# First attention by head with rounded scores and value products, its output product in two rounded halves, and a rounded convolution output

## The reference, cut to what matters

```python
h = rms_norm(x, g_mix);  u = h @ w_in                      # split: u_f, u_q, u_kv, u_kr
y_f = fourier_mix(u_f, w_fourier)                          # 1024 x 512
q = rms_norm(u_q) @ w_q_up                                 # 8 heads of 96 (32 of them rotated)
k, v = rms_norm(u_kv) @ w_kv_up, with the rotated u_kr     # 8 heads of 96 and of 64
s = q @ k.T * scale;  p = softmax(s);  o = p @ v           # per head, 1024 x 1024 scores
x = x + concat([y_f, o], -1) @ w_out                       # 1024 x 1024
x = x + memory_cross_attention(...);  x = x + expert_choice_moe(...);  x = rms_norm(x)
```

```python
u = glu_a * sigmoid(glu_b);  u = conv31(u) + b
u = silu(layernorm(u));  y_conv = (u * silu(z_conv)) @ w_conv_out
merged = sigmoid(g_conv) * y_conv + sigmoid(g_att) * y_att
x = x + gate * (merged @ w_o);  return rms_norm(x)
```

## Time and profile before

| | |
|---|---|
| median of 3 runs | 3215.53 us (3215.28 to 3217.62) |
| the profiled execution | 3215.87 us |
| its span | 3214.1 us |
| mean granted TensorE clock | 0.976 of full speed |
| busy: PE, DVE, ACT, POOL | 94%, 53%, 32%, 15% |
| first attention, first score product to last output product | 298.6 to 714.7 us |
| four groups of `yc` products | from 2932.6 to 3107.8 us, 27.47 us each |

### The profile page before, as it was taken

One profiled execution on the slowest core, in us unless ns is written; L12 is line 12 of the kernel. 1 busy time (PEld: TensorE's weight loads), 2 busy tenths in 40 slices (PEclk: granted clock), 3 DMA queues, 4 the chain that ended last, 5 costly groups with the idle time before them and its releaser, 6 DMA issues.

```text
span 3214.1 us, 34166 instructions
## 1 busy us (share of the span) xinstructions
PE 3034.9 (94%) x13636; PEld 2197.6 (68%) x13636; DVE 1701.7 (53%) x2367; ACT 1033.3 (32%) x1640; POOL 475.7 (15%) x426
## 2 busy tenths in 40 slices
PE   6999999989999899999996896999999999999998
PEld 3566666656466448888885684887877768676568
DVE  2323323321023278888885589677778966111144
ACT  2123323221021037777775300334343343000001
POOL 1310000000000121121113423000001144121031
PEclk9999999999999899999998897999999999999999
DMA  3011000012011289999996111002021131011121
GB/s 120 27 54 53 1 1 1 1 66 105 27 53 46 102 318 382 397 391 398 397 392 234 66 60 58 8 11 89 14 89 31 31 102 51 28 49 44 40 105 66
DMA packets 136985, 362.22 MB, mean 113 GB/s; under 512 B 11119, under 2 KB 43377, under 8 KB 136700
## 3 DMA queue, kind: packets, MB, share of 16 engines
q1 hardware_dynamic: 120860, 305.30, 25.2%
q0 software_dynamic: 14672, 50.48, 4.9%
...
...
## 4 chain that ended last, share of the span: by engine, by line
PE 84%; DVE 11%; ACT 1%; issue 1%; POOL 1%; DMA 1%; SPq 0%; POOLq 0%; DVEq 0%; ACTq 0%
PE ps L1899 29%; PE ps L1885 6%; PE ps L2157 5%; PE ps L2159 5%; PE ps L2158 5%; DVE b_f L1667 5%; PE ps L2172 5%; PE ps L2173 5%; PE ps L2174 5%; PE ps L1998 3%; PE ps L2009 3%; PE ps L2227 3%; PE ps L2228 2%; PE ps L2229 2%; PE ps L2263 2%
## 5 line engine op out<-in xcount | busy, mean ns | idle before, releaser
L1667 DVE SCALAR_TENSOR_TENSOR b_f<-b_f,small_f 128x1023 f32<-128x1023 f32 (+14 forms) x210 | 309.9, 1476 | 7.6 <-DVE small_f L1765 1.2
L1899 PE MATMUL ps<-w_f,ht_f 128*128 128x512 f32 (+1 forms) x768 | 299.0, 546 | 0.0
L1899 PEld LDWEIGHTS ps<-w_f,ht_f 128*128 128x128 f32 x768 | 168.4, 231 | 115.0 <-issue 88.5
L1899 PE MATMUL ps<-w_f,b_f 128*128 128x512 f32 (+1 forms) x544 | 235.0, 586 | 12.5 <-DVE x_f L1516 6.2
L1899 PEld LDWEIGHTS ps<-w_f,b_f 128*128 128x128 f32 x544 | 102.6, 193 | 130.9 <-issue 109.2
L2158 PE MATMUL ps<-w_f32r,a_f32r 128*128 128x512 f32 x456 | 177.9, 390 | 0.0
L2172 PE MATMUL ps<-x_f32r,w_f32r 128*128 128x512 f32 x416 | 164.8, 396 | 0.0
L2173 PE MATMUL ps<-ht_f32r,w_f32r 128*128 128x512 f32 x416 | 162.5, 391 | 0.0
L2174 PE MATMUL ps<-x_f32r,w_f32r 128*128 128x512 f32 x416 | 162.4, 390 | 0.0
L1885 PE MATMUL ps<-small_f 128*128 128x128 f32 (+1 forms) x728 | 106.4, 293 | 59.1 <-DVE small_f L1415 39.7
L1129 ACT ACTIVATE b_f<-ps,small_f 128x1024 f32<-128x1024 f32 x64 | 71.3, 1113 | 275.0 <-DVE small_f L1500 275.0
...
## 6 DMA issues: line engine op xcount, KB each, us to landing
...
```

The costliest lines, as they stand in the source:

```text
L1667: ins = v.scalar_tensor_tensor(C[:, k, d:S], U[k][:, 0:S - d], cols[:, k, R_TAP + j:R_TAP + j + 1], C[:, k, d:S], ALU.mult, ALU.add)
L1899: ins = mm(o, lhs(k), rhs(k), start=(k == 0), stop=(k == n - 1))
```

## The change

Steps of the first attention become n = 8h + t, head by head, and its products rounded:

- Scores are three rounded passes for each half of 512 keys; hi and lo of Q and K of the next head are made in the loop, hi by ACT at t = 2 and 4 (`head_hi`), lo by POOL at t = 3 and 5 (`head_lo`).
- DVE takes a reciprocal of the row sum in each step, and POOL multiplies the probabilities (128 x 1024, in place) by it before PE turns them. ACT copies the turned probabilities as hi, DVE subtracts for lo, two of 512 columns each.
- The value product serves two query tiles at once: 16 rounded matmuls of 256 columns with the 128-wide pair (V hi, V lo) of a head stationary; the two halves of the result are added by an ACT copy (`o_half`) and a DVE addition into `mixa`. ACT makes hi (`mix_hi`) and POOL (the last quarter DVE) lo of `mixa`; hi and lo of the attention half of the output weights are made in the loop by ACT and POOL at i = 34 to 41.
- The output product is cut: `y1f`, the Fourier half, right after `yf` and before kv (16 tiles of 12 rounded passes), added to X; `y1`, the attention half, after the loop (16 of 12 passes). X is written to DRAM after `y1f`, since V's pairs lie in its place, and read back after the last value product.
- `yc` becomes `product3`: four more weight slots (`co`) split on POOL, C's hi by ACT (16 copies of 128 x 512) and lo by DVE (16 subtractions). All `gc` products now stand before all `yc`, the sigmoids are kept.
- The first two splits of the second block, `gb0` and `ga0`, go from POOL to an ACT copy and a DVE subtraction.

```diff
-    for n in range(-1, NS + 1):
-        if n + 1 < NS:
-            yield "s", n + 1
-        if 0 <= n < NS:
-            yield "pt", n
-        if n - 1 >= 0:
-            yield "pv", n - 1
-            if (n - 1) % H1 == 2 and n - 1 > H1:
-                yield "y", (n - 1) // H1 - 1
-    yield "pv_end", 0
-    yield "y", T - 1
+    for i in range(-2, NS + 1):
+        if i + 2 < NS:
+            yield "s", i + 2
+        if 0 <= i < NS:
+            yield "pt", i
+        if i >= 2 and i % 2 == 0:
+            yield "pv", i // 2 - 1
...
+GC = CH[:12] + [(6, 0), (7, 0), (6, 1), (7, 1)]
+for nm, order in (("gc", GC), ("yc", CH)):
+    for c, h in order:
+        bk.add((nm, c, h))
...
+V_all = mem_r(X0, 8192).rearrange("p (t h d) -> p t h d", t=T, h=H1)
...
+        if w[0] == "mkv0":
+            for t in range(T):
+                bk.read(sp, ("y1f", t, 0)), bk.read(sp, ("y1f", t, 1))
+                sp.dma_start(dram["x1"][tile(t), :], X[:, t, :]).then_inc(sem(f"x_tile{t}"), 16)
+            bk.wait(sp, ("s1", 2 * T - 1))
+            for i in range(2):
+                sp.dma_start(mem(WO_AT[2 * i], 2048).rearrange("p (k n) -> p k n", k=2), w_mix[1][:, 2 * i:2 * i + 2, :]).then_inc(sem("wo_in"), 16)
+            bk.wait(sp, ("pt", NS - 1, 1))
+        elif w[0] == "mkv1":
+            bk.wait(sp, ("o1", NS // 2 - 1))
+            for t in range(T):
+                sp.wait_ge(sem(f"x_tile{t}"), 32)
+                sp.dma_start(X[:, t, :], dram["x1"][tile(t), :]).then_inc(sem(f"x_tile{t}"), 16)
+            bk.wait(sp, ("y1", T - 1, 1))
         fetch(n, w)
         if n == 0:
...
+        if i + 1 < NS:
+            n = i + 1
+            pool.wait_ge(sem("a_rec"), n + 1)
+            nc.gpsimd.tensor_scalar(pexp[n % 4], pexp[n % 4], rrec[:, n:n + 1], None, ALU.mult).then_inc(sem("p_norm"), 1)
+        h, t = divmod(i, T)
+        if h + 1 < H1 and i >= 0 and t in (3, 5):
+            pool.wait_ge(sem("head_hi"), 2 * (h + 1) + (t - 3) // 2 + 1)
+            whole, hi, lo = head_parts("kq"[(t - 3) // 2], h + 1)
+            nc.gpsimd.tensor_tensor(lo, whole, value(hi), ALU.subtract).then_inc(sem("head_lo"), 1)
...
-    split("gb0")
-    split("ga0")
...
+        if c == 2:
+            w_wait(act, "outf")
+            for k in range(4):
+                nc.scalar.activation(wf_hi[:, k, :], wview("outf")[:, k, :], ACT.Copy).then_inc(sem("out_hi"), 1)
...
+        act.wait_ge(sem(f"x_tile{t}"), 32)
...
+    def head_hi(nm, h):
+        whole, hi, lo = head_parts(nm, h)
+        nc.scalar.activation(hi, whole, ACT.Copy).then_inc(sem("head_hi"), 1)
...
+    for i in range(-1, NS + 2):
+        if i + 1 < NS:
+            n = i + 1
             act.wait_ge(sem("a_max"), n + 1)
...
+        if 0 <= i < NS:
+            m = i // 2
+            if i % 2 == 0 and m >= 2:
+                bk.wait(act, ("o1", m - 2))
...
+    def conv_hi(h):
+        for k in range(KC):
+            nc.scalar.activation(C_hi[h][:, k, :], C[:, k, NB * h:NB * h + NB], ACT.Copy).then_inc(sem("conv_hi"), 1)
+    for n, (c, h) in enumerate(GC):
         b = bk.wait(act, ("gc", c, h))
-        act.wait_ge(sem("tmp_used"), 16 + n - 3)
-        bk.done(nc.scalar.activation(tmp[n % 4], PS[:, b, :], ACT.Sigmoid), ("gc", c, h))
+        bk.done(nc.scalar.activation(gate_sig[2 * c + h], PS[:, b, :], ACT.Sigmoid), ("gc", c, h))
+        if (c, h) == (7, 0):
+            act.wait_ge(sem("tmp_used"), 16)
+            conv_hi(0)
+    conv_hi(1)
...
+        for h in range(2):
+            dve.wait_ge(sem("psum_hi"), 2 * c + h + 1)
...
+            bk.done(v.tensor_tensor(lo, b4(b), value(hi), ALU.subtract), ("yf", c, h))
+        if c == 2:
+            for k in range(4):
+                dve.wait_ge(sem("out_hi"), k + 1)
+                v.tensor_tensor(wf_lo[:, k, :], wview("outf")[:, k, :], value(wf_hi[:, k, :]), ALU.subtract).then_inc(sem("block1_lo"), 1)
...
+    def head_low(nm, n):
+        dve.wait_ge(sem("head_hi"), n)
+        whole, hi, lo = head_parts(nm, 0)
+        v.tensor_tensor(lo, whole, value(hi), ALU.subtract).then_inc(sem("block1_lo"), 1)
...
-                bk.done(v.tensor_tensor(x, x, PS[:, b, :], ALU.add), ("y1", n, j))
+            v.reciprocal(rrec[:, n:n + 1], rsum[:, n:n + 1]).then_inc(sem("a_rec"), 1)
+        if 0 <= i < NS:
+            for j in range(2):
+                dve.wait_ge(sem("p_hi"), 2 * i + j + 1)
+                b = bk.at[("pt", i, j)][0]
+                hi, lo = (x[i // 2 % 2][:, 4 * j:4 * j + 4, tile(i % 2)] for x in (pt_hi, pt_lo))
+                bk.done(v.tensor_tensor(lo, b4(b), value(hi), ALU.subtract), ("pt", i, j))
+        if i >= 3 and i % 2:
+            m = (i - 3) // 2
+            h, rows_, other, qs = heads_of(m)
+            dve.wait_ge(sem("o_half"), m + 1)
+            b = bk.at[("o1", m)][0]
+            bk.done(v.tensor_tensor(mixa[rows_, h // 2, qs], PS[rows_, b, 0:256], o_half[m % 2][rows_, :], ALU.add), ("o1", m))
+    dve.wait_ge(sem("mix_hi"), 4)
+    v.tensor_tensor(mixa_lo[:, 3, :], mixa[:, 3, :], value(mixa_hi[:, 3, :]), ALU.subtract).then_inc(sem("block1_lo"), 1)
...
+    for h in range(2):
+        for k in range(KC):
+            dve.wait_ge(sem("conv_hi"), KC * h + k + 1)
+            v.tensor_tensor(C_lo[h][:, k, :], C[:, k, NB * h:NB * h + NB], value(C_hi[h][:, k, :]), ALU.subtract).then_inc(sem("conv_lo"), 1)
...
         b = bk.wait(dve, ("yc", c, h))
...
+                pe.wait_ge(sem("head_lo"), 2 * h)
             b = bk.begin(pe, ("s1", n))
-            for j in range(2):
-                ins = mm(PS[:, b + j, :], QT[:, h, tile(t)], KT[:, h, NB * j:NB * j + NB], start=True, stop=True)
+            q1, q2 = q_hi[h % 2][:, tile(t)], QT_lo[:, h, tile(t)]
+            for j in range(2):
+                c = slice(NB * j, NB * j + NB)
+                mm(PS[:, b + j, :], q1, k_hi[h % 2][:, c], start=True, stop=False)
+                mm(PS[:, b + j, :], q1, KT_lo[:, h, c], start=False, stop=False)
+                ins = mm(PS[:, b + j, :], q2, k_hi[h % 2][:, c], start=False, stop=True)
             bk.end(ins, ("s1", n))
...
+        else:
...
+                mm(PS[:, b, 0:256], V_all[:, k, h, :], pt_hi[n % 2][:, k, :], start=(k == 0), stop=False)
+                ins = mm(PS[:, b, 0:256], V_all[:, k, h, :], pt_lo[n % 2][:, k, :], start=False, stop=(k == 7))
+            bk.end(ins, ("o1", n))
+    def mixed(t, j, k):
+        w1, w2 = (x[k][:, NB * j:NB * j + NB] for x in (wo_hi, wo_lo))
+        o = PS[:, bk.at[("y1", t, j)][0], :]
+        mm(o, mixa_hi[:, k, tile(t)], w1, start=(k == 0), stop=False)
+        mm(o, mixa_hi[:, k, tile(t)], w2, start=False, stop=False)
+        return mm(o, mixa_lo[:, k, tile(t)], w1, start=False, stop=(k == 3))
+    pe.wait_ge(sem("wo_lo"), 4)
+    pe.wait_ge(sem("mix_lo"), 3)
+    for t in range(T):
+        for j in range(2):
+            bk.begin(pe, ("y1", t, j))
+            for k in range(3):
+                mixed(t, j, k)
+        if t == 0:
+            pe.wait_ge(sem("block1_lo"), 7)
+        for j in range(2):
+            bk.end(mixed(t, j, 3), ("y1", t, j))
     for m in range(2):
...
             else:
                 split_wait(f"{nm}{c // 2}")
                 feature_major((nm, c, h), f"{nm}{c // 2}", c % 2, h, ht_2)
-    for i in range(4):
-        split_wait(f"gc{i}")
-        for c, h in CH[4 * i:4 * i + 4]:
-            feature_major(("gc", c, h), f"gc{i}", c % 2, h, ht_2)
-        w_wait(pe, f"co{i}")
-        pe.wait_ge(sem("tmp_used"), 16)
-        for c, h in CH[4 * i:4 * i + 4]:
-            product(("yc", c, h), lambda k: wview(f"co{i}")[:, k, tile(c % 2)], lambda k: C[:, k, NB * h:NB * h + NB], KC)
+    for c, h in GC:
+        split_wait(f"gc{c // 2}")
+        feature_major(("gc", c, h), f"gc{c // 2}", c % 2, h, ht_2)
+    for c, h in CH:
+        split_wait(f"co{c // 2}")
+        if c == 0:
+            pe.wait_ge(sem("conv_lo"), KC + KC * h)
+        wv = split_views(f"co{c // 2}")
+        product3(("yc", c, h), lambda k: [x[:, k, tile(c % 2)] for x in wv], lambda k: (C_hi[h][:, k, :], C_lo[h][:, k, :]), KC)
```

More of the change, by code:

```diff
@@ L777, in _ @@
                 if i >= RING:
-                    bk.wait(sp, post[i - RING][4])
+                    bk.wait(sp, post[before[n_post + i] - n_post][4])
+                if w[0] == "wo2":
+                    bk.wait(sp, ("yc", 7, 1))
+                    sp.wait_ge(sem("x4_out"), 16 * T)
+                    for t in range(T):
+                        sp.dma_start(XB[:, t, :], dram["x4"][tile(t), :]).then_inc(sem(f"x_tile{t}"), 16)
+                    sp.wait_ge(sem("tmp_used"), 32)
                 sp.dma_start(wview(w[0]), w[1]).then_inc(w_full[wslot(n_post + i)], 16)
@@ L1121, in _, with mix_round @@
                         copy(("qt", t - 1, j), QT[:, 4 * j:4 * j + 4, tile(t - 1)], b4(b)[0:HD1], scale=HD1 ** -0.5)
-            for kind, n in att1_steps():
-                if kind == "s":
+                if t == 4:
```

(57 more changed lines are left out.)

311 lines of the change are left out of this document (173 added, 138 removed).

## The result

The changed kernel takes 3228.77 us (median of 6 runs, 3225.35 to 3232.84) where the kernel before takes 3216.22 (6 runs, 3214.51 to 3217.62): ratio 1.0039, 95% interval 1.0026 to 1.0052. It is slower by 0.4%, about twice what the measurement can tell. The forecast was 3128, with 3083 to 3175 as its range. The profiled execution took 3232.84 us, 4.1 over its median.

What follows compares the result with a forecast made beforehand. TensorE, busy 94% of the span, was taken to bound the kernel, with the loop's engines now in a ring. Attention region -62.3, convolution output -22.2, between blocks -2.7: -87.2 from 3215.87, so 3128 us; range 3083 to 3175.

Steps and rivals of the forecast that it cites:

- which puts 1024 at 1.09: Attention loop: POOL's multiplication of 1024 columns takes 1.09 us, worked out from its tensor-scalars of 512 and 2048 columns.
- The ring: Attention loop: PE, DVE and POOL wait in a circle; 6.96 us a pair of steps, PE waiting 0.56, 222.7 in all.
- The heads' ends: Attention loop: a head's first scores wait for POOL's lo of Q, 3.75 us more, seven times, 26 in all.
- The clock: Attention loop: short idles lower TensorE's clock somewhat; 3 us added.
- rival D: Attention loop: idle in every pair lowers TensorE's clock to 1.2 GHz, total 3282, slower; decides if over 57% of loop; chance 0.06.
- B: Attention loop: POOL's multiplication with a scalar per row costs 2.34 us, +1.25 a pair, total 3171; chance 0.17.
- Rival C: Attention loop: the queues overlap and PE's 205 us is the loop, 50 less, about 3083; chance 0.10.
- Around the loop: Before and after the attention loop: `y1f` and `y1` 43.5 us each, plus 4.2, 2.3 and 1.3 of waits.
- The convolution output: Second block's `yc`: 16 products of 24 rounded passes, 87.2 us against 109.9; with 0.5 of wait, -22.2.
- The stall that was feared: Convolution output: DVE's subtraction from SBUF stalls while POOL splits a `co` slot; up to 5 us.
- Between the blocks: Second block's start: POOL's split no longer holds its row scale, -2.7 us.
- The forecast's other estimate for this operation, 1.54 us: POOL's multiplication by the Trainium skill's 1.8 cycles an element: 1.54 us, making the loop some 14 us longer.

Runs made afterwards that it cites:

- e1: Changed kernel with a constant 1.0 for POOL's scalar per row, division left out: multiplication 2770 ns, total 17.8 us over the kernel before.
- e5: Changed kernel with an addition of 0.0 after POOL's multiplication in the same instruction: loop 279.7 us, total 69.8 us under the kernel before.
- e13: e5 with passes of no use in PE's waits, two at even steps, twelve at a head's start: loop 268.5 us, total 74.2 under the kernel before.
- e4: Changed kernel with DVE's reciprocal ahead of the next step's maximum: loop 295.5 us, total 3167.67 us, 45.7 under the kernel before.
- e3: Changed kernel with passes of no use in PE's waits, seven at even steps, fourteen at a head's start: loop 333.5 us, total 3206.63 us.
- e11: Changed kernel with e5's and e4's edits, next head's hi and lo two steps earlier, POOL's other subtractions apart: 3085.92 us, ratio 0.9598 to the kernel before.
- e10: Changed kernel with the convolution output as f32 products of the hi parts again: 3249.57 us, 34.0 over the kernel before.

## Why the prediction was wrong, step by step

- **The step that failed** is "which puts 1024 at 1.09": the price of POOL's multiplication. It measured 2.843. The sentence took care of the operand (a scalar per row) and bounded the price by the two-source operation, 2.34; e1 shows that the operand is worth 0.07. Every tensor-scalar in the earlier trace rows has two operations, and the change's has one; the truth lay outside both ends. With a second operation (e5: 1.127, and pairs of 7.0) the price is right to 0.04 us, and the loop falls by 77 of the 100 us by which it was too long.
- **The ring** was right: DVE's order, PE's wait once a pair, 8.71 worked out with the measured price and 8.72 seen. What the sum lacked is the loop's filling and emptying, 5.5 us in e13. e4 moved one instruction and took 61 us out of the loop.
- **The heads' ends** were right in place (PE's wait ended by POOL's lo of Q) and nearly in size, 3.75 forecast and 3.9 in e13 (10.88 - 6.96), with 0.4 or more in the pair behind it that the sum didn't have. With the slow form they cost more, since a multiplication stands ahead of each subtraction and behind it.
- **The clock** was priced at 3 us and as rival D. It was at half for 119 us of the loop (33%, not the 57% that D needed), and the passes of e3 brought 23.5 us of the loop back. Even with the quick multiplication it costs 11 us (e5 against e13), not 3. Rivals B and D were taken as cases that exclude each other, but B's longer wait brings D about in part. With both, the kernel came out slower than before; with one of them it wouldn't have: e3, the slow form at a clock of 0.97, stands 6.7 us under the kernel before (one execution, so hardly clear of it), and e5, the quick form at 0.89, 69.8 under.
- **Rival C** (PE's floor is the loop) was a fair picture of what the kernel could do: e11 comes to 3085.92. Its own figure has a slip: 50 less than 3128 is 3078, not the 3083 that became the range's lower end; the miss doesn't hang on it.
- **Around the loop**: the first scores came 2.4 us later than forecast (in part because TensorE is at half for 3.4 us at the start of `y1f`), `y1` took 43.7 for 43.5.
- **The convolution output** gave 20.3 by the traces and 21.4 by e10, for 22.2. `yc` itself takes 88.1 us, 87.7 forecast with its 0.5 of wait (PE waited 0.76). Why the whole second block gave 1.5 less than that stage did, no run shows. DVE's subtractions for C's lo stayed at 0.7, but by luck of time: none of the 16 ran beside a subtraction of POOL. The stall that was feared did come, at another place: DVE's rounding copies of the merged values (L2021, from SBUF to SBUF) take 0.43 us, and four of the 16 took 4.71 beside POOL's subtractions of 4.9; PE waited for none of them. The operation of the earlier trace rows is an addition (L1825), not a subtraction as the forecast has it. Between the blocks: 1.8 for 2.7.
- The forecast's other estimate for this operation, 1.54 us, was worked out from the 1.8 cycles an element of the Trainium skill (GPSIMD Engine Reference, section 3.1 Elementwise). The runs show 1.13 in one form and 2.84 in the other, so it held for neither. The Trainium skill (TensorE: Matmul & The Clock Gate, Part 4: PE-mode transpose) says that transposes don't count as busy in the same way, from which the forecast read that the clock would fall. In e11 about a quarter of PE's time is transposes (0.88 of each 3.24 us) and the granted clock is 0.99, and e3 brings the clock back with the transposes left as they are. So here the idle time decides, not the transposes.
